# Linear attention in one stage, semaphores of stages without clears, and an earlier multiplication in the attentions

## What is computed

```python
q_in, k_in, k_end = qc * exp(b), kc * exp(-b), kc * exp(b_last - b)
a_intra = where(lower, einsum('bhncd,bhnsd->bhncs', q_in, k_in), 0)
o_intra = einsum('bhncs,bhnse->bhnce', a_intra, vc)
chunk_state = einsum('bhnsd,bhnse->bhnde', k_end, vc)
state = dec[..., None] * state + chunk_state      # by chunks, s_enter = state before
o = o_intra + einsum('bhncd,nbhde->bhnce', q_in, s_enter)
y_gla = rms_norm(o_forward + flip(o_backward), norm_g) * silu(g)
```

## Time and profile before

| | |
|---|---|
| median of 3 runs | 4702.76 us (4702.31 to 4703.58) |
| profiled execution | 4678.14 us, its span 4676.4 us |
| TensorE busy in the span | 4156.1 us (89%) |
| VectorE, ScalarE, GpSimd busy | 2244.5, 1479.2, 665.8 us |
| mean granted clock of TensorE | 0.945 |

### The profile page before, as it was taken

One profiled execution on the slowest core, in us unless ns is written; L12 is line 12 of the kernel. 1 busy time (PEld: TensorE's weight loads), 2 busy tenths in 40 slices (PEclk: granted clock), 3 DMA queues, 4 the chain that ended last, 5 costly groups with the idle time before them and its releaser, 6 DMA issues. The chain is left out here.

```text
span 4676.4 us, 59875 instructions
## 1 busy us (share of the span) xinstructions
PE 4156.1 (89%) x23580; PEld 3534.6 (76%) x23580; DVE 2244.5 (48%) x4183; ACT 1479.2 (32%) x2393; POOL 665.8 (14%) x578
## 2 busy tenths in 40 slices
PE   6997586787999999999999898679999989768998
PEld 5775476666888888888888777458888878658997
DVE  2142444432788554677766554444333335344444
ACT  2232353222333333322222342352211234153222
POOL 0000052100277874001010000000000000000000
PEclk8998788898999999999999999899999999789999
DMA  2212000532466677987877211001111111002222
GB/s 94 81 43 82 1 1 1 179 109 92 136 142 142 140 176 184 292 268 263 265 265 261 98 51 37 30 24 64 63 59 63 54 60 59 10 30 91 95 95 73
DMA packets 257181, 499.69 MB, mean 107 GB/s; under 512 B 121936, under 2 KB 123856, under 8 KB 256144
## 3 DMA queue, kind: packets, MB, share of 16 engines
q1 hardware_dynamic: 205200, 445.51, 30.3%
q0 software_dynamic: 51712, 50.49, 5.0%
HBM read 426.57 MB, written 69.34 MB: 106 GB/s over the span
## 5 line engine op out<-in xcount | busy, mean ns | idle before, releaser
L431 PE MATMUL psum<-h_hi,w_hi 128*128 128x258 f32 (+2 forms) x2176 | 699.0, 321 | 54.3 <-DVE w_lo L397 31.0
L431 PE MATMUL psum<-h_lo,w_hi 128*128 128x258 f32 (+2 forms) x2176 | 693.4, 319 | 0.0
L431 PE MATMUL psum<-h_hi,w_lo 128*128 128x258 f32 (+2 forms) x2176 | 693.3, 319 | 0.0
L2095 DVE TENSOR_TENSOR ex_w_lo<-ex_raw,ex_w_hi 128x1024 fp32r<-128x1024 f32 x256 | 313.5, 1225 | 413.7 <-ACT ex_w_hi L1949 401.8
L1826 POOL DMA_INDIRECT gates<-gate,cell x256 | 440.1, 1719 | 327.9 <-DVE gate L2052 195.9
L431 PEld LDWEIGHTS psum<-h_hi,w_hi 128*128 128x128 f32 x2176 | 414.8, 191 | 93.0 <-issue 31.3
L431 PEld LDWEIGHTS psum<-h_lo,w_hi 128*128 128x128 f32 x2176 | 414.6, 191 | 32.2 <-issue 1.4
L431 PEld LDWEIGHTS psum<-h_hi,w_lo 128*128 128x128 f32 x2176 | 414.6, 191 | 29.1
L1949 ACT ACTIVATE ex_w_hi<-ex_raw 128x1024 fp32r<-128x1024 f32 x256 | 270.2, 1056 | 481.9 <-PE psum L1906 481.9
L1878 PE MATMUL psum<-xn_ffn_hi,ex_w_hi 128*128 128x512 f32 x1024 | 403.7, 394 | 4.2 <-DVE ex_w_lo L2095 4.2
L1879 PE MATMUL psum<-xn_ffn_lo,ex_w_hi 128*128 128x512 f32 x1024 | 399.4, 390 | 0.0
(11 more groups left out here) (447 smaller groups left out, 7382.6 us busy)
## 6 DMA issues: line engine op xcount, KB each, us to landing
ex_raw<-in_peer_u SPq DMA_DIRECT2D x128, 512.0 KB
ex_raw<-in_peer_v SPq DMA_DIRECT2D x128, 512.0 KB
peer_qk<-in_w_mod SPq DMA_DIRECT2D x96, 512.0 KB, 5.1
gelus<-gelu SPq DMA_DIRECT2D x128, 256.0 KB
small<-gates POOLq DMA_DIRECT2D x128, 256.0 KB, 5.0
peer_qk<-gelus SPq DMA_DIRECT2D x128, 256.0 KB, 4.0
w_raw<-in_w_in SPq DMA_DIRECT2D x48, 512.0 KB, 3.4
w_raw<-in_w_gate SPq DMA_DIRECT2D x44, 512.0 KB, 3.3
```

Of the source, the lines that this page charges most:

```text
L431: last = nc.tensor.matmul(o, a, b, start=(begins and i == 0 and j == 0), stop=(ends and i == len(todo) - 1 and j == len(pairs) - 1))
L2095: V.tensor_tensor(w_lo[:, n % PARTS, :], raw[:, n % RAW, :], w_hi[:, n % PARTS, :].bitcast(F32), ALU.subtract)\
```

## The change

**Semaphores.** Stages take numbers from a range of 132 in turn. They are cleared, with one barrier, only when the range is used up; rings of transfers have 12 numbers of their own. In rmsnorm GpSimd now waits at its end for its own last operations (`pooled`).

**Linear attention.** The seven stages become one, so that 12 stage ends are gone. The state walk reads PSUM directly. TensorE takes the tiles' inner products and the 16 transposes of values between the steps of the walk. Window copies of values (`v_win`) and queries (`q_blk`) and the gate's multiplication go to GpSimd. The four loads are issued at the start, bias last; ScalarE takes the silu of the gate first and waits after two transposes for all four loads to scale the gate by the norm's weights. The output sums alternate between the array's halves, both into one bank. The norm takes 2-column sums per tile, and root and reciprocal are of 8 to 16 columns.

**Attentions.** The multiplication into `y` stands ahead of the two reductions of its iteration.

```diff
--- before.py
+++ after.py
-def clear(k, sems):
-
-    nums = sorted(s.num for s in sems)
-    while nums:
-        n = next((i for i in range(1, len(nums)) if nums[i] != nums[0] + i), len(nums))
-        k.nc.all_engine_barrier(sems_to_clear=range(nums[0], nums[0] + n))
-        nums = nums[n:]
+class Numbers:
...
+    STAGES, RINGS = 132, 12
+
+    def __init__(self, nc):
+        self.nc = nc
+        free = sorted(nc.free_semaphores)
+        want = self.STAGES + self.RINGS
+        first = next(n for n in free[::-1] if set(range(n, n + want)) <= set(free))
+        self.first, self.last = first, first + self.STAGES
+        self.at, self.ring_at = self.first, self.last
+        self.ring_last = self.last + self.RINGS
+
+    def take(self, n):
+        if self.at + n > self.last:
+            self.nc.all_engine_barrier(sems_to_clear=range(self.first, self.at))
+            self.at = self.first
+        self.at += n
+        return range(self.at - n, self.at)
...
+        sems = [cx.enter_context(k.nc.semaphore(n, num=num))
+                for n, num in zip(names, k.numbers.take(len(names)))]
         with k.nc.Block(no_gpsimd_drain=True) as block:
             yield (block, *sems)
-        clear(k, sems)
...
-        clear(k, ring.arrived)
...
+                            .then_inc(pooled, 1)
+                pool.wait_ge(pooled, len(order) // 2)
...
+                if 0 <= s - LAG - 2 < N:
+                    v = s - LAG - 2
+                    dve.wait_ge(rows_kept, v + 1)
+                    o = pairs[v]["out"]
+                    got, by = ps[:, OUT, 0:P], inv_rows[:, :]
+                    if len(o.shape) == 3:
+                        got, by = (x.rearrange("p (a b) -> p a b", a=o.shape[1]) for x in (got, by))
+                    nc.vector.tensor_tensor(o, got, by, ALU.mult).then_inc(done, 1)
                 if s < N:
...
-                if 0 <= s - LAG - 2 < N:
-                    v = s - LAG - 2
-                    dve.wait_ge(rows_kept, v + 1)
-                    o = pairs[v]["out"]
-                    got, by = ps[:, OUT, 0:P], inv_rows[:, :]
-                    if len(o.shape) == 3:
-                        got, by = (x.rearrange("p (a b) -> p a b", a=o.shape[1]) for x in (got, by))
-                    nc.vector.tensor_tensor(o, got, by, ALU.mult).then_inc(done, 1)
...
+    STATE, INNER, TURN, OUT, SPREAD_TO = (0, 1), (2, 3), (4, 7), (5, 6), (0, 1, 2)
...
+            params = [(norm_g[:, :], io["gla_norm"][layer, :, :]),
+                      (win.sink[:, :], io["swa_sink"][layer, :, :]),
+                      (masks[:, 0:3 * P], io["swa_mask"]),
+                      (bias[:, 0:win.n_bias, :], io["na_bias"][layer, :, :, :])]
+            for dst, src in params:
+                sp.dma_start(dst, src).then_inc(loaded, 16)
+            sp.wait_ge(loaded, 16 * len(params))
...
+            for b in range(NA_BLOCKS):
+                if b == 3:
...
+                    nc.gpsimd.tensor_copy(
+                        v_win[b][f].rearrange("p (r c) -> p r c", c=NA_CB),
+                        grid_of(proj, TV_NA + f, slice(0, P), win.starts[b], NA_CB))\
+                        .then_inc(v_moved, 1)
...
+                        .then_inc(q_moved, 1)
+            pool.wait_ge(gated, FT)
+            for t in range(n_out):
+                pool.wait_ge(out_kept, t + 1)
+                tok = slice(t * P, (t + 1) * P)
+                nc.gpsimd.tensor_tensor(o[:, :, tok], o[:, :, tok], gate[:, :, tok], ALU.mult)\
+                    .then_inc(times, 1)
...
+            for i in range(CHUNKS):
+                if i < STEPS:
+                    for f in range(FT):
+                        for d in range(2):
+                            r = d * FT + f
+                            t, half = divmod(walk[d][i], P // C)
+                            rows = slice(half * C, (half + 1) * C)
+                            if f == 0:
+                                wait_from(pe, walked, R * (i - 1) + FT * (d + 1))
+                            for hp in range(2):
+                                last = nc.tensor.matmul(
+                                    ps[HALVES[hp], STATE[d], f * HD:(f + 1) * HD],
+                                    k_end[r][rows, t * P + hp * HD:t * P + (hp + 1) * HD],
+                                    v_tok[rows, t, f, HALVES[hp]], start=True, stop=True)
+                    last.then_inc(states, 1)
+                t = i // 2
+                if i % 2 == 0 and t < n_out:
+                    tok = slice(t * P, (t + 1) * P)
+                    wait_from(pe, masked, 4 * t)
+                    for r in range(R):
+                        for hp, rows in enumerate(HALVES):
+                            last = nc.tensor.matmul(ps[:, INNER[hp], r * P:(r + 1) * P],
+                                                    k_in[rows, r, tok], q_in[rows, r, tok],
+                                                    start=True, stop=True)
+                    last.then_inc(inner, 1)
+                for j in range(i * len(jobs) // CHUNKS, (i + 1) * len(jobs) // CHUNKS):
+                    _, srcs, blocks = jobs[j]
+                    wait_from(pe, turn_kept, j - 1)
+                    wait_from(pe, v_moved, blocks)
+                    for a, src in enumerate(srcs):
+                        last = nc.tensor.transpose(ps[:, TURN[j % 2], a * P:(a + 1) * P], src,
+                                                   k.ident)
+                    last.then_inc(turned, 1)
...
+                    pe.wait_ge(kept, t + 1)
+                    wait_from(pe, out_kept, t - 1)
+                    wait_from(pe, squared, t - 1)
+                    bank = OUT[t % 2]
+                    for f in range(FT):
+                        for hp, rows in enumerate(HALVES):
+                            nc.tensor.matmul(ps[rows, bank, f * P:(f + 1) * P],
+                                             v_tok[:, t, f, rows], a_sb[:, t, hp, f, :],
+                                             start=True, stop=False)
+                        for d in range(2):
+                            for half in range(P // C):
+                                j = t * (P // C) + half
+                                at = f * P + half * C
+                                for hp, rows in enumerate(HALVES):
+                                    last = nc.tensor.matmul(
+                                        ps[rows, bank, at:at + C], entry[rows, j, d * FT + f, :],
+                                        q_in[rows, d * FT + f, j * C:(j + 1) * C],
+                                        start=False, stop=(d == 1 and half == P // C - 1))
+                    last.then_inc(out_ready, 1)
+                if t:
+                    v = t - 1
+                    lot = 0 if v < LOTS[0][1] else 1
+                    pe.wait_ge(squared, v + 1)
+                    pe.wait_ge(turn_kept, len(jobs))
+                    for f in range(FT):
+                        at = (v - LOTS[lot][0]) * HEADS + 2 * f
+                        last = nc.tensor.matmul(ps[:, TURN[lot], at:at + 2],
+                                                sq[:, f, v * P:(v + 1) * P],
+                                                k.ones_half[:, 0:P:HD], start=True, stop=True)
+                    last.then_inc(summed, 1)
...
+            nc.scalar.activation(gate, gate, ACT.Silu).then_inc(silued, 1)
+            for j, (dst, srcs, _) in enumerate(jobs):
+                act.wait_ge(turned, j + 1)
+                nc.scalar.activation(dst, ps[:, TURN[j % 2], 0:len(srcs) * P], ACT.Copy)\
+                    .then_inc(turn_kept, 1)
+                if j == 1:
+                    act.wait_ge(loaded, 64)
+                    act.wait_ge(silued, 1)
+                    for f in range(FT):
+                        nc.scalar.activation(gate[:, f, :], gate[:, f, :], ACT.Identity,
+                                             scale=norm_g[:, f:f + 1]).then_inc(gated, 1)
...
+                act.wait_ge(out_ready, t + 1)
+                got = ps[:, OUT[t % 2], 0:FT * P].rearrange("p (a b) -> p a b", a=FT)
+                nc.scalar.activation(o[:, :, t * P:(t + 1) * P], got, ACT.Copy)\
+                    .then_inc(out_kept, 1)
+                nc.scalar.activation(sq[:, :, t * P:(t + 1) * P], got, ACT.Square)\
+                    .then_inc(squared, 1)
...
+                    dve.wait_ge(states, i + 1)
+                    wait_from(dve, walked, R * i)
+                    for d in range(2):
+                        c, nxt = walk[d][i], walk[d][i + 1]
+                        for f in range(FT):
+                            r = d * FT + f
+                            nc.vector.scalar_tensor_tensor(
+                                entry[:, nxt, r, :], entry[:, c, r, :], edges[:, r, c:c + 1],
+                                ps[:, STATE[d], f * HD:(f + 1) * HD], ALU.mult, ALU.add)\
+                                .then_inc(walked, 1)
...
+                if i % 2 == 0:
```

(72 more changed lines are left out.)

433 lines of the change are left out of this document (155 added, 278 removed).

## The result

The changed kernel takes 4512.81 us (4509.47 to 4513.62, 4 runs) against 4703.17 us (4702.31 to 4704.55, 4 runs) for the kernel before: a ratio of 0.9594, 95% interval 0.9577 to 0.961. In a later measurement it took 4511.8 us beside 4701.1.

What follows compares the result with a forecast made beforehand. Operation chains and stage ends were taken to bound linear attention half the time, TensorE the attentions. Clears 29 + linear attention 88.8 + attentions 36 - clock 4 = 150 us off 4678.1, plus 24.6, gave 4552 us; range 4524 to 4597.

Steps and rivals of the forecast that it cites:

- The carry from the profile to the median: Whole kernel: the sum is made against the profiled 4678.14 us, and 24.6 us are added to reach the median.
- (c): Output tiles of linear attention: 3.3 us a tile, 19.8 us in layer 0 and 13.2 us in layer 1.
- (a): Start of the linear-attention stage: ScalarE waits for all loads, bias last, so TensorE goes on at 14.5 us.
- (b): Other eight walk steps of linear attention, in pairs: 18.8 us in layer 0, 15.4 us in layer 1.
- (d): Tail of linear attention, from last square through sums, root and reciprocal to one product: 5.5 us a layer.
- Attentions: Value sums of both attentions: the earlier multiplication into y recovers 36 of 39.7 us TensorE idle time, bounds 0 to 39.7.
- Clears: Stage boundaries outside linear attention: 70 clears go at 0.414 us each, 29 us gained, bounds 26 to 30.5.
- Clock behind the one stage: Start of the attentions, behind linear attention's tail: TensorE at the lower clock costs 4 us in all, bounds 0 to 8.
- 1: Linear attention: alternated outputs sharing one bank do not overlap, about 50 us more, 4602 us; chance 0.13.
- 2: Attentions: the wait passes on to ScalarE's copies or exponentials, 28 us less gain, 4580 us; chance 0.10.
- 3: Stage boundaries: clears cost nothing, as engines would stand there anyway, 29 us less gain, 4581 us; chance 0.03.
- 4: Attentions and following feed-forward networks: TensorE's clock stays at 1.2 GHz, making the kernel slower, 4777 us; chance 0.02.

## Why the prediction was wrong, step by step

**The carry from the profile to the median: the step that failed.** "I make the sum against 4678.14 and add 24.6 at the end." That is right only if the distance between profile and median is the same in both kernels. Here it was no constant: it was the clock of one stage, layer 0's outputs, at 0.94 in the profiled execution and, by the mean clocks of whole executions and the two profiles of its neighbours, near 0.5 in most others; and the change replaced that very stage. Both other kernels that ran that stage without the new order show it (56.30 and 60.40 us), and those that alternate its products have one level. 21 of the 39 us that the forecast missed are this: with the 3.3 us of the new kernel in place of 24.6 the forecast would have been 4532, and a range as wide around it would have held 4512.8. Against the profiles alone the sum of 149.8 missed 18.9 us: linear attention 16.6 and the attentions with their clock 6.3 too little, clears 4.0 too much.

**Linear attention, (c), mis-sized.** The forecast was 3.3 us a tile, a middle between two clocks with a division by 1.6. The products with alternation took half the time, 1.96 us a tile instead of 3.8 at the same clock, and the clock was 1.00. With the norm's small sums a tile is 2.5 us. Outputs and first spreads: 15.6 and 10.5 us, forecast 21.2 and 14.6, so 9.7 us. "Its clock will be low" was the wrong half of the argument: in the rest of the walk TensorE was busy 16.33 of 17.29 us, and from 2910 on the clock was 1.00.

**Linear attention, the rest, right.** (a) TensorE went on at 13.7 and 14.2 us, forecast 14.5, by the mechanism named: ScalarE behind the bias. (b) 17.3 and 14.0 us, forecast 18.8 and 15.4. (d) the tail 4.5 and 3.6 us, forecast 5.5. Together 51.0 and 42.4 instead of 60.0 and 50.0: the gain of 105.4 us is within the bounds of 32 to 106 that were given, at their edge, while the total's range was cut closer. GpSimd's copies of 128x256 took 0.35 to 0.51 us, where 0.3 to 1.35 had been allowed (no row stood behind the 0.3), and TensorE waited for none of them.

**Attentions, right.** 38.3 us, forecast 36 of 39.7. Put back alone, 39.0.

**Clears, right in kind.** 25.0 us outside linear attention, forecast 29. Four wide clears took 0.7 to 0.8 us instead of 0.05, which the count had not: 2.7 of the 4. In the kernel before all 87 were worth 33 to 35 of the 36 counted.

**Clock behind the one stage, mis-sized.** 4 us had been set aside. The outputs left the clock at 1.00, and the attention of layer 0 kept it (1.00 over its 114.50 us). In layer 1 it fell for a moment, behind the tail in which TensorE had little to do:

```profile
3970.00:3973.00 3.00, 3.00 (x16) 2.40 (x15) 1.81 (x5) 1.82 (x5) 0.00 (x0) 0.50 0.00 0
```

Three microseconds at the lower level cost some 1.3 us, by estimate from the factor 1.75 of the earlier trace rows. So the term was worth some 1.3 us in one layer and nothing in the other.

**Rivals.** 1 (no overlap) did not occur here. The kernel that really lacks the alternation is 42 us slower, 51 in the profile, where 50 stood, but that agreement is partly luck: a tile's sums took 6.6 us there (four times 1.66) as the rival had it, while the tile they are held against takes 2.5 and not 3.3 us, and the longer pairs, 16 of the 50, did not come. Its reason, one bank for both halves, is refuted by the kernel with two banks, which takes the same time. The prediction's argument against it was no evidence: in the walk of the kernel before each chunk has a bank of its own (`j % 8`) and uses one half of the array's rows, so that walk never had two row halves in one bank. The Trainium skill ("TensorEngine Tiling (Array Packing)", Restrictions and Gotchas, Gotcha 1) says that different row tiles can't access the same PSUM bank simultaneously; no run here shows a time that comes from that rule, since one bank and two gave 4511.8 and 4513.8 us. 2, 3 and 4 are out by the runs above.

**The range.** Its lower end had room for each piece to be a few us better, and none for the baseline to be on another level.

## What to carry to other kernels

Before adding a difference between profile and median to a forecast, find out which stage holds it: here two levels of time with two mean clocks came from one stage that ran at either clock, and the change to that stage took the level away. Small products that use a quarter or half of the array are worth trying in an order that alternates between halves; here that halved their time, and the clock was part of the gain. Where one engine's list holds a wait for a large transfer, give the small transfer that it really needs its own semaphore.

## What the runs showed of the hardware

- With TensorE busy without a gap, but with products that stayed in one half of the array through half a tile of the outputs, the clock fell from 1.00 to 0.50 in one kernel (0.68 to 1.11 us for eight records), never rose from 0.50 in another, and in the profile of before stayed at 1.00 for some 26 us. With the same products alternating it was 1.00 through the outputs in the profiles of the changed kernel.
- Alternating 64x64 products of the two halves took 0.042 us for each record of the trace instead of 0.084, alike in one bank and in two (0.68 us for sixteen).
- A clear of a few numbers took 47 ns in the median, one of over 100 numbers 695 to 805 ns; the barrier around a small one brings it to 0.41 us.
- GpSimd copied 128x256 in about 0.35 us (nine in 3.13, VectorE busy for 0.86 of them), at the lower end of what was bounded; three later copies took 0.51 us each, which no run explains. It multiplied 128x256 in 0.72 us.
- The same stage, unchanged, ran at a mean clock of 0.94 in two profiles of the kernel before and at 0.53 and 0.50 in profiles of two kernels that differ from it elsewhere; the kernel before as a whole takes 4678 or 4700 us.
